# The last expert matrix of a mixture-of-experts kernel, issued by GpSimd in sixteen 8-row transfers instead of by SyncE in one

## What is computed

```
def hierarchical_moe(h, w_group, b_group, w_expert, b_expert, w1, w3, w2):
    """Top-1 expert group, then top-2 experts within it; experts are SwiGLU MLPs."""
    ...
    def run_block(args):
        toks, wts, e = args
        xb = x_pad[toks]
        hid = jax.nn.silu(xb @ w1[e]) * (xb @ w3[e])
        return (hid @ w2[e]) * wts[:, None].astype(xb.dtype)
```

## Time and profile before

| | |
|---|---|
| Median of 3 runs | 1557.46 us (1556.17 to 1557.83) |
| The profiled execution | 1556.8 us, its span 1554.8 us |
| TensorE's granted clock, mean | 0.994 |
| Matmuls (PE) busy | 1434.5 us (92%) |
| VectorE, ScalarE, GpSimd busy | 628.2, 508.2, 0.2 us |
| Read from HBM, written | 493.98 MB, 1.05 MB |

### The profile page before, as it was taken

How to read it: one execution, slowest core, us unless ns; L and a number is a source line. 1 busy time by engine, 2 the same in 40 slices (tenths; PEclk the granted TensorE clock), 3 DMA queues, 4 the chain that set the end, 5 groups by cost and what they waited for, 6 DMA issues and landing times.

```text
span 1554.8 us, 23249 instructions
## 1 busy us (share of the span) xinstructions
PE 1434.5 (92%) x9825; PEld 907.1 (58%) x9825; DVE 628.2 (40%) x1489; ACT 508.2 (33%) x1112; POOL 0.2 (0%) x4
## 2 busy tenths in 40 slices
PE   7999999999999999899999998888888888888887
PEld 7778877788878888544444444434434344344332
DVE  6886687678547567422222222122122121121111
ACT  6676657676557655101111111000010110100102
POOL 0000000000000000000000000000000000000000
PEclk9999999999999999999999999999999999999999
DMA  8434443533443586999999999999999999999995
GB/s 293 162 109 149 182 146 109 188 129 111 165 165 109 195 292 241 398 424 427 428 428 426 427 428 425 428 427 427 428 427 427 427 428 426 428 427 427 427 427 237
DMA packets 71550, 496.60 MB, mean 319 GB/s; under 512 B 6256, under 2 KB 10640, under 8 KB 46352
## 3 DMA queue, kind: packets, MB, share of 16 engines
q1 hardware_dynamic: 71440, 495.05, 77.9%
HBM read 493.98 MB, written 1.05 MB: 318 GB/s over the span
## 4 chain that ended last, share of the span: by engine, by line
PE 61%; DMA 33%; DVE 3%; ACT 2%; issue 1%; SPq 0%; DVEq 0%; ACTq 0%
DMA arena<-in_expert_w 27%; PE ps L1137 25%; PE ps L1526 7%; PE ps L1533 6%; DMA tenth<-in_expert_w 6%; PE ps L1553 4%; PE ps L1564 4%; PE ps L1134 3%; PE ps L1507 2%; PE ps L1248 1%; PE ps L1117 1%; PE ps L1168 1%; DVE arena L2124 1%; PE ps L1576 1%; ACT arena L1678 1%; PE ps L1480 1%
## 5 line engine op out<-in xcount | busy, mean ns | idle before, releaser
L2121 DVE COPY arena<-ps 128x512 f32<-128x512 f32 (+3 forms) x210 | 115.5, 574 | 480.3 <-PE ps L1526 388.8
L1681 ACT ACTIVATE arena<-ps 128x512 f32<-128x512 f32 (+6 forms) x245 | 120.6, 498 | 544.1 <-PE ps L1553 308.1
L1526 PE MATMUL ps<-arena 128*32 128x512 f32 x1840 | 221.8, 600 | 66.2 <-DMA arena<-in_expert_w 66.2
L1533 PE MATMUL ps<-arena 128*128 128x512 f32 x504 | 251.2, 621 | 0.5 <-DVE arena L2121 0.5
L1681 ACT ACTIVATE w_hi<-arena 128x512 fp32r<-128x512 f32 (+3 forms) x328 | 194.3, 614 | 147.3 <-PE ps L1137 119.9
L2124 DVE TENSOR_TENSOR w_lo<-arena,w_hi 128x512 fp32r<-128x512 f32 (+3 forms) x312 | 196.8, 658 | 97.5 <-ACT w_hi L1681 96.3
L1564 PEld LDWEIGHTS ps<-arena 128*128 128x128 f32 x1024 | 129.3, 192 | 85.6 <-issue 82.7
L1137 PE MATMUL ps<-w_hi,hT_hi 128*128 128x512 f32 (+3 forms) x448 | 172.7, 385 | 3.2 <-DVE w_lo L2124 2.3
L1137 PE MATMUL ps<-w_hi,hT_lo 128*128 128x512 f32 (+3 forms) x448 | 166.3, 371 | 0.0
L1137 PE MATMUL ps<-w_lo,hT_hi 128*128 128x512 f32 (+3 forms) x448 | 166.0, 371 | 0.0
L1526 PEld LDWEIGHTS ps<-arena 128*32 128x32 f32 x1840 | 50.8, 109 | 191.4 <-DMA arena<-in_expert_w 105.6
(11 more groups left out here) (174 smaller groups left out, 1442.2 us busy)
## 6 DMA issues: line engine op xcount, KB each, us to landing
arena<-in_expert_w SPq DMA_DIRECT2D x172, 2048.0 KB, 45.9
arena<-in_w_in SPq DMA_DIRECT2D x24, 2048.0 KB, 7.8
tenth<-in_expert_w SPq DMA_DIRECT2D x20, 2048.0 KB, 44.7
arena<-in_w_out SPq DMA_DIRECT2D x8, 1024.0 KB, 6.6
arena<-in_w_mem_kv SPq DMA_DIRECT2D x2, 2048.0 KB, 10.7
arena<-in_w_branch_hgrn SPq DMA_DIRECT2D x2, 2048.0 KB, 13.4
arena<-in_w_out SPq DMA_DIRECT2D x2, 2048.0 KB, 13.2
arena<-in_w_branch_mla SPq DMA_DIRECT2D x2, 2048.0 KB, 8.7
```

The lines of the kernel that those rows point to most:

```text
L1526: o = e.matmul(B[32 * j:32 * j + 32, :], Xs[:, k, q:q + 32], Wn[:, k, :], start=i == 0, stop=i == 1)
L1533: i = e.matmul(acc[t][h][:, :], CT[ex % 2][:, t * 128:t * 128 + 128], Ys[:, h * 512:h * 512 + 512], start=False, stop=False)
L1681: return e.activation(o, i, ACTF.Copy, scale=scale)
L2121: return e.tensor_copy(o, i)
```

## The change

The loop of SyncE stops at matrix 190. A new program for GpSimd waits for the same event as SyncE did (the reader of matrix 181), and then issues matrix 191 in sixteen DMAs of 8 rows of 16 KB each. Ahead of each stands a DMA of 8 rows of 16 bytes from the constants into a new, otherwise unused tensor `spare`. The sixteen data transfers add 256 to a new semaphore, `s_last`, and the readers of matrix 191 wait for that. Nobody waits for `s_spare`.

```diff
         flagi = ctx.enter_context(nc.sbuf_tensor("flagi", [1, 1], I32))
+        spare = ctx.enter_context(nc.sbuf_tensor("spare", [128, 64], F32))
...
+        s_last, s_spare = sem("s_last"), sem("s_spare")
...
         def expert_landed(m):
             s = RING[m % NR]
+            if m == 3 * NE - 1:
+                return s_last, 256
             return s_w[s], 16 * (EARLY[s] + m // NR + 1)
...
-            for m in range(3, 3 * NE):
+            for m in range(3, 3 * NE - 1):
                 expert(m)
...
-        for engine in (tensor, scalar, vector, sync):
+        def gpsimd(e):
+
+
+            m = 3 * NE - 1
+            ex, which = matrix_of(m)
+            assert which == 2
+            src = A["expert_w2_2"][0, ex].rearrange("(p k) n -> p (k n)", k=4)
+            w = Waits(e)
+            w.wait_ge(*at("expert", m - NR))
+            for i in range(16):
+                rows = slice(8 * i, 8 * i + 8)
+                e.dma_start(spare[0:8, 4 * i:4 * i + 4], A["cst"][0:8, 4 * i:4 * i + 4]).then_inc(s_spare, 16)
+                e.dma_start(slots[RING[m % NR]][rows, :], src[rows, :]).then_inc(s_last, 16)
+
+        for engine in (tensor, scalar, vector, sync, gpsimd):
             engine(Nothing())
...
         block.sync(sync)
+        block.gpsimd(gpsimd)
```

## The result

The changed kernel takes 1593.36 us in the median (1590.26 to 1595.27) against 1557.64 us of the kernel before: the ratio is 1.023, with a 95% interval of 1.0217 to 1.0243. That is 35.7 us more. The forecast was 10 us more. The time is in the stated range and at the place of rival B.

What follows compares the result with a forecast made beforehand. The prediction took a loading stage at 424 to 428 GB/s, its end set by matrix 190, as the bound. Terms of 9.8 us for added packets and 0.3 us for tiny transfers gave +10 us, 1567.5 us, range 1560 to 1602 us.

Steps and rivals of the forecast that it cites:

- rival B: GpSimd's writes into SBUF: four neighbouring rows share one way, 2.46 us a packet, ending at 1596.8 or 1590 us; chance 0.28.
- part 1: SyncE's queue: one DMA less to issue, 0.41 us, worth nothing because a later wait hides it.
- part 2: GpSimd's start: it waits for the reader of matrix 181, so issuing still starts at about 1493.4 us.
- part 3: GpSimd's 32 issues: taken at 1 us each, upper bound 2 us, ending before 1535.9 us.
- Part 4: Matrix 191 in its own queue: lands early, by about 1530 us, which buys nothing as TensorE needs 190 first.
- Part 5: Queue ahead of matrix 190: eight engines get 16 packets each at 0.614 us, so 190 lands late, +9.8 us.
- The question of the late and the early half: Which eight DMA engines carry matrix 191: late-finishing ones give 1567.5 us, chance 0.30; early-finishing ones 1561 us, chance 0.21.
- A: DMA engines: the early half carries matrix 191, so 190 is only 3.0 to 3.6 us late, 1561 us; chance 0.21.
- Part 6: Tiny transfers and completion posts on the engines: taken as 0.3 us, between 0 and 3.2 us.
- C: GpSimd is slow: at 2 us per issue matrix 191 comes late, +18 us, 1575 us; chance 0.07.
- E: DMA engines serve GpSimd's queue only once SyncE's is empty: 190 on time, no change, 1557.5 us; chance 0.07.
- D: Even spread: the eight engines change between transfers, 8 packets more on each, 4.9 us, 1562.4 us; chance 0.07.

Runs made afterwards that it cites:

- low half: Changed kernel with rows 4 apart and only its first eight transfers (rows 0 to 63), the rest of matrix 191 not loaded: 1561.59 us, ratio 1.0026.

## Why the prediction was wrong

**What bounds the kernel** was right. Matrix 190 decides and 191 does not, and the 13.7 us behind it moved unchanged. Nothing speaks against part 1; part 2 was right (GpSimd's first issue is at 1492.6 us), part 3 too high (0.51 us an issue instead of 1), without effect. Part 4 was right on its worth, nothing. The landing of 191 was far off: by the completion posts the fifteenth transfer was through at 1563.8 us, not by 1530 us, and the sixteenth was only issued after it.

**Part 5 failed, on its price**: "eight engines get 16 packets each: 16 x 0.614 = 9.8 us". The eight engines are shown, and that they are always the same (by the posts below). The 0.614 us is not what such a packet takes: it took 1.10 us in the mean, and SyncE's own packets, which the sum left at their old price, went to 1.00 us. 0.614 us is the price of a packet when every engine writes its usual rows (0.61 us in the low half), and I carried it over from a stage in which nothing else happens. The runs put the price together like this; the last column is the last completion post of matrix 190 in the profiled execution, before 1535.9 us:

| rows of matrix 191 | over the kernel before | 190 landed, us |
|---|---|---|
| 128 rows in one transfer, 16 engines | +5.0 us | 1541.6 (+5.7) |
| 8 engines, rows 4 apart | +12.8 us | 1550.5 (+14.6) |
| 8 engines, rows 2 apart | +22.8 us | 1558.2 (+22.3) |
| 8 engines, neighbouring rows (the change) | +35.7 us | 1569.2 (+33.3) |

By W half of the rows 4 apart go through foreign ways. In the first two profiled executions `down` of expert 62 ran at a granted clock of 0.50 at first and took 3.55 and 3.36 us instead of 1.92 us; that is TensorE's and not the packets', so the last column is the cleaner one.

The second line is near to the forecast's 10 us, so about a third of the result comes with eight engines and rows 4 apart, and the 22.9 us between it and the last line are the choice of neighbouring rows. **Rival B** is what happened: it gave 1596.8 or 1590 us. It had 0.28, hardly less than the forecast, and its argument was the Trainium skill, "SBUF — State Buffer", section "Door 1: The DMA port swizzle": four neighbouring partitions behind one port, 27.6 GB/s for partitions 0 to 3. By that rule 1, 2 and 4 rows of a transfer share a port, and the order of the rates agrees with it (421, 329 and 244 GB/s). I ranked it behind because the trace did not show it; but the trace of before could not have shown it, as it has no transfer of that kind. With the trace silent, the measured figure of the Trainium skill was the only evidence, and it should have led.

B's working was simpler than the chip. It has every software packet at four times 0.614 us, 39.3 us in all, and SyncE's at their old speed. In the trace the changed kernel's 128 software packets take 1.10 us in the mean and 2.08 us at the most, and SyncE's 16 KB packets between 1497 and 1550 us 1.00 us in the mean instead of 0.62. An estimate from these means for an engine with both is 16 x 1.10 = 17.6 us, and 723 / 16 = 45 packets of SyncE's with 0.38 us more each, another 17 us: 35 us, and the landing of 190 moved by 33.3 us in that execution. By this estimate half of the loss lies in SyncE's own packets. The posts of 190 show it too: eight engines carry no rows of 191, and yet none of the 16 is through with 190 before 1540.7 us, while before half of them were by 1529.4 us and all by 1535.9 us. What slows them, an engine's other queue or guests on its way, the trace doesn't tell apart.

**The question of the late and the early half** had neither answer. The 16 completion posts of matrix 190, sorted, in us from the span's start, show it; they are read from the trace's semaphore events, before and in the run with the low half:

```
before    1525.3 1525.3 1525.5 1525.7 1526.6 1526.8 1527.2 1529.4 1534.4 1534.5 1534.6 1534.9 1534.9 1535.1 1535.5 1535.9
low half  1525.5 1526.4 1530.1 1530.2 1530.8 1531.5 1531.9 1534.0 1534.3 1534.3 1534.8 1535.1 1535.4 1535.8 1539.6 1540.0
```

Before there are eight early and eight late engines, as the share in the earlier trace rows told. In the low half two posts of the early group stay, six are some 5 us later, six of the late group stay, and two are over 4 us later. Eight transfers over changing engines would have moved all sixteen. So the eight engines with data are always the same, six early and two late, and those two set the landing. The last engine paid the full price, as the forecast had it for the late half, and A's condition, data on early engines alone, did not hold. That instruction loads make the late ones late was not tested and stays an estimate.

Part 6: the tiny transfers cost nothing that shows. No row shows a cost for part 7. **C** did not occur, nor did **E**: GpSimd's first data packet runs at 1497.2 us, 4 us after its issue, beside a full queue of SyncE's. **D** is what one 128-row transfer gives, 1562.6 us against 1562.4 us worked out.

No run beat the kernel before. By the chain of before none could on this route, since matrix 191 stands behind 190 there and nothing is gained by having it sooner; the best that loads all of it adds 5 us.

## What to carry to other kernels

When a loading stage runs at full rate, ask of every added transfer which engines write which partitions, not only how many bytes it has: the same 2 MB cost 5 us as 128 rows and 36 us as sixteen times 8 neighbouring rows. A transfer that skips ahead of a full queue delays everything in it; check what is waited for next, not whether the skipped matrix lands early. And look at the DMA share together with the rate: a share near 1 with a rate that fell from 427 to 244 GB/s meant here that packets of the same size took longer.

## What the runs showed of the hardware

- What a packet into SBUF takes depends on its partition and on the engine that writes it. Rows 4 apart among 0 to 63, eight engines: 0.61 us per 16 KB packet in the mean, beside a full SyncE queue. Rows 64 to 127 by the same engines: 0.97 us. Neighbouring rows: 1.10 us, up to 2.08 us. Without the tiny transfers between them 1.30 us. Ways that are shared by partition are the reading that fits all of these; for neighbouring rows the pieces in HBM were not varied by themselves.
- Such transfers slow the other queue too: SyncE's packets go from 0.62 to 1.00 us in the mean (1497 to 1550 us), and the DMA share stays between 0.98 and 1.05 from 1500 to 1540 us. It needs no second queue: with SyncE alone its packets went from 0.62 to 1.00 us from 1525 us on.
- A GpSimd transfer of 8 whole rows always puts its data on the same eight engines (in the low half eight of the 16 posts of 190 stay and eight move), and transfers put in between steer nothing (1593.4 us with them, 1597.7 us without). Cut into two pieces per row, the transfers reach all 16 engines (all 16 posts move by some 5 us), and their order counts: 1562.3 us against 1575.9 us. The Trainium skill has both forms, some direct copies laid out over all 16 engines and consecutive engines from a cursor, in "DMA: Bandwidth & Descriptors", section "Why a DMA increments its semaphore by 16 and not by 1", and the runs with whole rows agree with the first, those with pieces with the second.
- GpSimd issues such a transfer in 0.52 us. With 32 of them the last one was held back for 55.9 us, until 1564.4 us, just after the fifteenth data transfer was through (1563.8 us); with 16 none was. Why was not tested.
